# Layer tail of a hybrid decoder trunk: separate products, norms and MLP against one program that goes chunk by chunk

## The reference, cut to what matters

```python
x = x + g1 * rms_norm(m, norm_g[l, 1])                 # m = mixer output @ w_out
h = rms_norm(x, norm_g[l, 2]) * (1 + sc2) + sh2
x = x + g2 * rms_norm(jnp.square(relu(h @ w1)) @ w2, norm_g[l, 3])
# the next layer begins: h = rms_norm(x, norm_g[l+1, 0]) * (1 + sc1) + sh1;  h @ w_in
```

## Time and profile before

| What | us |
|---|---|
| Median of three runs | 3804.24 |
| The profiled execution, its own time | 3808.08 |
| Span of its trace, first to last instruction | 3806.4 |
| Product with `w_out`, layer 0 (1281.9 to 1380.0) | 98.1 |
| Norms behind it (1380.0 to 1473.1) | 93.1 |
| MLP of layer 0 (1473.1 to 2266.1) | 793.0 |
| Norms behind it (2266.1 to 2358.8) | 92.7 |
| Norms behind the `w_out` product of layer 1 | 93.4 |
| Final norm and output (3750.6 to 3806.4) | 55.8 |

### The profile page before, as it was taken

One profiled execution on the slowest core, in us unless ns is written; L12 is line 12 of the kernel. 1 busy time (PEld: TensorE's weight loads), 2 busy tenths in 40 slices (PEclk: granted clock), 3 DMA queues, 4 the chain that ended last, 5 costly groups with the idle time before them and its releaser, 6 DMA issues. The chain is left out here.

```text
span 3806.4 us, 43764 instructions
## 1 busy us (share of the span) xinstructions
PE 3190.1 (84%) x17509; PEld 2794.1 (73%) x17509; DVE 1407.3 (37%) x1513; ACT 880.2 (23%) x1083; POOL 761.3 (20%) x422
## 2 busy tenths in 40 slices
PE   4988888699587766999999984979693899999996
PEld 2973333299365666999999983958393899999996
DVE  4026641101693345322322335139316332232234
ACT  3016642100321213111111122013303111111112
POOL 1111111111000132211221223225023222122121
PEclk7999989899796777999999995989695999999997
DMA  5110025310432112111111111130312111111112
GB/s 198 56 51 8 1 72 178 116 50 28 132 95 75 50 53 86 41 42 44 44 39 44 44 64 71 43 108 0 100 33 94 56 44 39 44 44 39 44 44 94
DMA packets 216088, 238.36 MB, mean 63 GB/s; under 512 B 7779, under 2 KB 173079, under 8 KB 214837
## 3 DMA queue, kind: packets, MB, share of 16 engines
q1 hardware_dynamic: 210229, 219.14, 17.9%
q0 software_dynamic: 5120, 16.78, 1.4%
q10 hardware_dynamic: 656, 1.36, 0.1%
HBM read 207.74 MB, written 29.99 MB: 62 GB/s over the span
## 5 line engine op out<-in xcount | busy, mean ns | idle before, releaser
L771 POOL TENSOR_TENSOR mlp_w_lo<-mlp_w_raw,mlp_w_hi 128x1024 fp32r<-128x1024 f32 x128 | 316.1, 2470 | 1250.6 <-ACT mlp_w_hi L748 1250.6
L614 PE MATMUL PS<-mid_x_hi,mlp_w_hi 128*128 128x364 f32 x1536 | 509.8, 332 | 46.3 <-POOL mlp_w_lo L771 46.3
L614 PE MATMUL PS<-mlp_h_hi,mlp_w_hi 128*128 128x364 f32 x1536 | 507.3, 330 | 40.7 <-DVE mlp_h_lo L820 40.7
L615 PE MATMUL PS<-mid_x_lo,mlp_w_hi 128*128 128x364 f32 x1536 | 505.9, 329 | 0.0
L615 PE MATMUL PS<-mlp_h_lo,mlp_w_hi 128*128 128x364 f32 x1536 | 505.5, 329 | 0.0
L616 PE MATMUL PS<-mlp_h_hi,mlp_w_lo 128*128 128x364 f32 x1536 | 504.7, 329 | 0.0
L616 PE MATMUL PS<-mid_x_hi,mlp_w_lo 128*128 128x364 f32 x1536 | 504.4, 328 | 0.0
L823 DVE TENSOR_TENSOR M<-M,PS 128x1092 f32<-128x1092 f32 x128 | 165.4, 1292 | 558.2 <-PE PS L616 558.2
L614 PEld LDWEIGHTS PS<-mid_x_hi,mlp_w_hi 128*128 128x128 f32 x1536 | 289.7, 189 | 46.8 <-issue 46.8
L614 PEld LDWEIGHTS PS<-mlp_h_hi,mlp_w_hi 128*128 128x128 f32 x1536 | 289.9, 189 | 45.6 <-DVE mlp_h_lo L820 45.6
L748 ACT ACTIVATE mlp_w_hi<-mlp_w_raw 128x1024 fp32r<-128x1024 f32 x128 | 134.8, 1053 | 691.3 <-PE PS L616 668.5
(11 more groups left out here) (373 smaller groups left out, 5643.0 us busy)
## 6 DMA issues: line engine op xcount, KB each, us to landing
mlp_w_raw<-mlp_w SPq DMA_DIRECT2D x128, 512.0 KB
M<-cache_sb_k SPq DMA_DIRECT2D x64, 256.0 KB, 3.1
big<-cache_sb_v POOLq DMA_DIRECT2D x64, 256.0 KB, 3.5
hgrn_pairs_ada_w<-ada_w SPq DMA_DIRECT2D x24, 512.0 KB
x_scratch<-big SPq DMA_DIRECT2D x2, 4368.0 KB
x_mid<-x_scratch SPq DMA_DIRECT2D x2, 4368.0 KB
x_scratch<-x_mid SPq DMA_DIRECT2D x2, 4368.0 KB
setup_ada_w<-ada_w SPq DMA_DIRECT2D x16, 512.0 KB, 7.2
```

Source lines behind the costliest of these rows:

```text
L614: pe.matmul(out, hi, xh, start=first, stop=False)
L615: pe.matmul(out, hi, xl, start=False, stop=False)
L771: pool.tensor_tensor(wl[:, u % 2, :], raw[:, u % 2, :], wh[:, u % 2, :].bitcast(F32), ALU.subtract).then_inc(s_lo, 1)
```

## The change

`mlp_of_layer`, the `residual_norm` behind the MLP and the `dense` for `odd_w_in` are replaced by one program per layer, `trunk`, without a barrier inside. Its order of work on PE is: the `w_out` product in two halves of four slices, each half chunk by chunk; then eight groups of hidden and output slices, each chunk by chunk; then, in layer 0, the product with `odd_w_in` in three parts of four slices, each chunk by chunk. Four weight tiles are resident (`w_hi`, `w_lo` have four slots), so that four slices of one chunk are computed before the next chunk. A slice of one chunk (`tile8`) is 24 pairs into one bank, an output slice of a chunk 12 pairs; six banks go round, and banks 6 and 7 hold the sums and the spread factors of the norms. The two norms of a chunk are issued between the products of later chunks (`norm_step`), at written places. ACT and DVE have one written order in which the steps of the norms stand between the copies, the hidden slices and the weights. `x` and the hidden slices share one memory, and so the old `x` is loaded in three chunks at the start, and each chunk of the new `x` is stored on ACT's queue.

The core of the diff:

```diff
-def mlp(nc, core, tag, w1, w2, M):
+def trunk(nc, core, tag, l, w_out, w1, w2, w_next=None):
+        wh = sb("w_hi", [P, 4, 8 * P], F32R)
+        wl = sb("w_lo", [P, 4, 8 * P], F32R)
+        freed_g = [9, 10, 11, 12, 30, 32, 34, 36]
...
+            for u in range(2):
+                load_tile(u, w_out, u * P)
+            for c in range(NC3):
+                sp.dma_start(col(X, c), col(x_rows, c)).then_inc(s_x[0][c], 16)
+            for u in range(2, 8):
+                load_tile(u, w_out, u * P)
+            with sp.Fori(0, G) as g:
+                load_group(g)
...
+            def sums(j, n, c):
+                pe.wait_ge(s_tree[j][n], 2 * (c + 1))
...
+                for k in range(2):
+                    for b in range(4):
+                        q = pe.matmul(PS[0:TB, 6 + n, SUM_AT + 4 * c + b:SUM_AT + 4 * c + b + 1],
+                                      sq[:, k, b * TB:(b + 1) * TB], cols(core, "ones"), ...
+            def spread(j, n, c):
+                pe.wait_ge(s_rs[j][n], c + 1)
...
+                if phase == 3:
+                    if s == 4:
+                        sums(j, 1, 1)
+                    if s == 5:
+                        spread(j, 1, 1)
+                    if s == 6:
+                        sums(j, 0, 2)
+                    if s == 7:
+                        spread(j, 0, 2)
...
+            def tile8(bank, slot, c, after=None):
+                for k in range(KT):
+                    q = product(pe, PS[:, bank, 0:CW], wh[:, slot, k * P:(k + 1) * P], wl[:, slot, k * P:(k + 1) * P],
+                                XH[:, k, c * CW:(c + 1) * CW], XL[:, k, c * CW:(c + 1) * CW], k == 0, k == KT - 1)
+                    if k == 3 and after is not None:
+                        after(0)
+                q.then_inc(s_mm, 1)
...
+            def hidden_phase(g, c, first=False, step=None):
+                for i in range(4):
+                    if c == 0:
+                        pe.wait_ge(s_lo, g * 8 + (8 + i + 1))
+                    if first and i == 0:
+                        pe.wait_ge(s_xl[0], 2 * (c + 1))
...
+            def down_phase(g, c, step=None):
+                for f in range(8):
+                    if f == 0:
+                        pe.wait_ge(s_h, g * 12 + 4 * (c + 1))
...
+            for c in range(NC3):
+                out_phase(0, c)
+            for c in range(NC3):
+                out_phase(1, c, lambda s: norm_step(0, c, s))
+            for c in range(NC3):
+                hidden_phase(0, c, True, lambda s: norm_step(0, 3 + c, s))
+            for c in range(NC3):
+                down_phase(0, c)
+            with pe.Fori(1, G - 1) as g:
...
+                act.dma_start(col(x_rows, c), col(X, c)).then_inc(s_st[j][c], 16)
...
-        mlp_of_layer(nc, core, 0, core.even_w_out, M)
...
+            trunk(nc, core, "trunk0", 0, core.even_w_out, core.mlp_w1[0], core.mlp_w2[0], core.odd_w_in)
             odd_mixer(nc, core, "odd")
...
+            trunk(nc, core, "trunk1", 1, core.odd_w_out, core.mlp_w1[1], core.mlp_w2[1])
```

More of the change, by code:

```diff
@@ L742, in _ @@
         @block.scalar
         def _(act):
[L744 to L772, removed]
@@ new lines, in group @@
+            def group(g):
+                for c in range(NC3):
+                    for i in range(4):
+                        hidden(g, c, i)
+            for c in range(NC3):
+                dve.wait_ge(s_sh, c + 1)
+                dve.tensor_tensor(col(XL, c), col(M, c), col(XH, c).bitcast(F32), ALU.subtract).then_inc(s_sl, 1)
+            tree(0, 0, 0)
+            recip(0, 0, 0)
+            scaled(0, 0)
+            residual(0, 0)
+            tree(0, 1, 0)
+            tree(0, 0, 1)
@@ new lines, in _ @@
+            recip(0, 1, 0)
+            normed(0, 0)
+            recip(0, 0, 1)
+            low(0, 0, 0)
+            low(0, 0, 1)
+            scaled(0, 1)
+            residual(0, 1)
+            hidden(0, 0, 0)
+            tree(0, 1, 1)
+            hidden(0, 0, 1)
+            tree(0, 0, 2)
+            hidden(0, 0, 2)
+            recip(0, 1, 1)
+            normed(0, 1)
+            recip(0, 0, 2)
+            hidden(0, 0, 3)
+            low(0, 1, 0)
+            low(0, 1, 1)
+            scaled(0, 2)
@@ new lines, in _ @@
+            residual(0, 2)
+            hidden(0, 1, 0)
+            tree(0, 1, 2)
+            hidden(0, 1, 1)
+            hidden(0, 1, 2)
+            hidden(0, 1, 3)
+            recip(0, 1, 2)
+            normed(0, 2)
+            low(0, 2, 0)
+            low(0, 2, 1)
+            for i in range(4):
+                hidden(0, 2, i)
+            for c in range(NC3):
+                for f in range(8):
+                    down(0, c, f, True)
+            with dve.Fori(1, G - 1) as g:
+                group(g)
+                for c in range(NC3):
+                    for f in range(8):
+                        down(g, c, f)
@@ new lines, in _ @@
+            tree(1, 1, 0)
+            down(e, 2, 0)
+            tree(1, 0, 1)
+            down(e, 2, 1)
+            recip(1, 1, 0)
+            down(e, 2, 2)
+            down(e, 2, 3)
+            normed(1, 0)
+            recip(1, 0, 1)
+            down(e, 2, 4)
+            down(e, 2, 5)
+            low(1, 0, 0)
+            down(e, 2, 6)
+            low(1, 0, 1)
+            down(e, 2, 7)
+            scaled(1, 1)
+            residual(1, 1)
+            tree(1, 1, 1)
+            tree(1, 0, 2)
```

564 lines of the change are left out of this document (488 added, 76 removed).

## The result

The changed kernel takes 3593.73 us (median of four runs, 3588.66 to 3604.74), the kernel before 3805.89 us beside it: a ratio of 0.944, 95% interval 0.9418 to 0.9461. The forecast was 3603. The profiled run took 3591.43 us with a span of 3589.8.

A forecast was written before the change was run, and what follows sets the result against it. PE was taken to bound the products, and a chain of ACT, DVE, POOL and small PE steps the norms. 40.7 + 52.0 + 52.3 + 46.5 + 19.6 - 15.4 + 5.4 = 201 us off 3804.2 gave 3603, range 3560 to 3650.

The forecast's parts named there:

- Wait in each group: In each of the MLPs' 16 groups PE waited 2.54 us for DVE's `mlp_h_lo`; this goes, saving 40.7 us.
- restarts: After long waits PE starts at half clock: 13 pairs at 0.308 instead of 0.168 us, 1.8 us each.
- Norms behind `w_out`, layer 0: Norms after layer 0's `w_out` product: 14.8 us small matmuls, 22.7 waits, 3.6 clock; 41.1 left of 93.1, 52.0 saved.
- Norms and next product: Norms behind the first MLP, interleaved with the next input product: 46.2 us left of 92.7, 46.5 saved.
- The end: Last norms and output of the kernel: 36.2 us left of 55.8, 19.6 saved.
- Start: earlier by: At each tail's start the first weight tile waits for one chunk's input copies, not all eight: 4.6 us earlier.
- Start: wait for the third weight: At each tail's start three x loads precede the third `w_out` tile on SP: PE waits 10.5 us per layer.
- Sum of the tails: All savings in both layers, less 15.4 us lost at the starts: 201 us.
- the norms did not hide: Rival: norm chains hide wholly beside products and x loads share the queue; 111 us less, 3492 us; chance 0.08.
- A new wait in each group: Rival: MLP weight tiles come late, so 2.5 us per group stay; 41 us more, 3644 us; chance 0.13.
- The clock at half through the stretches: Rival: PE's clock stays half through the three norm stretches; 145 us more, 3748 us; chance 0.09.
- It did not fall between sets: Rival: waits at bank changes drop the clock, output slices run at half; 645 us more, 4248 us; chance 0.04.

The follow-up runs named there:

- chunk 1 early: The changed kernel with chunk 1's second-norm root, reciprocal, high and low parts moved ahead in ACT's and DVE's queues: 3575.6 us, 0.9382 of before.
- all moves: The changed kernel with x loaded behind the fourth `w_out` tile, chunk 1's and 2's norm steps earlier, POOL's subtractions behind DVE's remainder: 3556.1 us, 0.9336 of before.
- the run with the two apart: The changed kernel, but before the next input product POOL's third and fourth weight tiles wait for DVE's remainder of chunk 0: 3602.1 us, one run.
- the run on the end: The kernel with all moves, plus DVE's last-norm sum with x of chunk 1 split and put behind the last addition: 3549.1 us, 0.9327 of before.

## Why the prediction was right

Its steps against the profiled run; a pair is 672.33 / 4032 = 0.1667 us, so 864 pairs take 144.1 and 288 take 48.0:

| Step | predicted | measured |
|---|---|---|
| Wait in each group | 40.7 saved | 16 x (98.9 - 96.05) = 45.6, with two restarts |
| Norms behind `w_out`, layer 0 | 41.1 left | 197.17 - 144.1 - 8.9 = 44.2 |
| Norms and next product | 46.2 left | 59.33 - 48.0 + 180.87 - 144.1 = 48.1 |
| The end | 36.2 left | 55.58 - 48.0 + 32.34 = 39.9 |
| Start: earlier by | 4.6 each | 14.86 - 9.80 = 5.1, and 5.1 |
| Start: wait for the third weight | 10.5 each | 4.71, and 6.18 in layer 1 |
| Sum of the tails | 201 saved | 207.1 |

(8.9 are the wait of 4.71 and the two restarts at the tail's start, 2.6 and 1.6.)

The waits inside the norms came out as summed from the rows: 1.38 (1), 2.33 (2.4), 6.38 (6.3), 2.33, 10.62 (10.6); in the next product 5.42 (5), 5.84 (5.8) and 10.63. Their causes are shown in part: the order in ACT's and DVE's queues by the runs with chunk 1 early and with all moves, POOL beside DVE by the run with the two apart. What is left before chunks 1 and 2 (3.1 and 8.6 us) is argued to be the chain's own length; no run shortened it. The group wait is shown by putting it back. It gave 4.9 us more than foretold; 3.0 of them are the two restarts, the rest is open.

Three terms were mis-sized. *The start* took 270 GB/s for the loads of x, between 192 and 355. They ran at 367; the second row is two weight tiles behind them in the queue:

```profile
1271.00:1279.00 8.00, 8.00 (x34) 8.00 (x34) 7.72 (x2) 3.15 (x2) 4.43 (x1) 0.67 1.06 367
...
1279.50:1282.50 3.00, 2.00 (x12) 1.69 (x11) 0.00 (x0) 0.00 (x0) 0.00 (x0) 1.00 1.16 295
```

The first row is x alone: its 2.93 MB went in 2044 packets, all but 30 of 1456 bytes. 4.47 MB then take 12.2 us and not 16.6, which takes 4.4 of the 10.5 us away; the value next to the faster row was the right one. The step that failed is the reading of 192 GB/s as the rate of 512-byte pieces: it is the mean of a window of 2.6 us in whose first half little moved (at most 142 GB/s), and in whose last third the same pieces moved at over 300. *The end* left out that DVE does chunk 1's sum with x, 4.15 us, before the last addition; the run on the end moves it, and the stretch comes to the 29 us foretold. *The norms* were too cheap, by 3.1 us behind `w_out` and 1.9 behind the MLP, though their waits were right. A restart was counted for the long waits only; behind the short ones, of 1.38 and 2.33 us, the clock stood at half too:

```profile
1395.80:1399.20 3.40, 3.30 (x12) 2.82 (x10) 1.79 (x2) 0.06 (x1) 0.00 (x0) 0.50 0.00 0
1402.60:1406.00 3.40, 3.40 (x14) 3.36 (x13) 3.40 (x7) 0.00 (x0) 0.00 (x0) 0.51 0.00 0
```

At the 1.5 us of a restart in the run with the wait put back, an estimate, these two make up the 3.1 us. The start was some 11 us too dear, the norms and the end some 12 too cheap. That the sum came within 6 us is in part luck; that it is near 200 is not.

The rivals: the norms did not hide. By moving entries in the queues the start's wait, the two waits before a spread, half of chunk 1's and a fifth of chunk 2's could be hidden, 45 us of the 111 foretold for that case. A new wait in each group did not come, even with POOL's work doubled. The clock at half through the stretches shows as short dips; the mean is 0.91 to 0.93 there. It did not fall between sets: 672 us at 1.00 with 24 more sets in each group. The section of the Trainium skill that spoke for that rival (TensorE: Matmul & The Clock Gate, "A second HAM failure mode: psum-queue depth-cycling") tells of small idle times between sets. This trace has none in the MLP (PE busy for 672.33 of 672.33 us), so that cycling through banks alone did not bring them about here.

## What to carry to other kernels

Where every wait of a written order can be named with the queue entries ahead of the waiting step, the waits can be summed from durations in the old trace, here to 0.1 us for most and 0.4 for the others. What went wrong here is a transfer's rate read from a window that holds its start, work that stands in a queue ahead of the last step, and the clock behind short waits. When a stage is interleaved, ask of each remaining wait whether it is the chain's length or the order of two queues: moving a few entries gave 17.5 us in the tails without a new instruction. Cut runs into stages before comparing: the part that the change left alone moved by 23 us between runs.

## What the runs showed that was not expected

- In the run with the wait put back, PE stood 2.3 us in each of 16 groups of work at full rate. Behind six of these waits the clock stood at 0.5 for a stretch, at 1.5 us each (13 pairs in 3.60 us, mean clock 0.55); behind the others it stayed at 1.00. The sum of waits is then too low a price.
- Beside POOL, DVE can slow down over a whole stage and not only where two instructions collide: with POOL's work in the MLP doubled, DVE's 336 instructions there took 286.4 us and not 179.5, and the eight of a remainder before it 14.86 and not 4.3.
- x in pieces of 1456 bytes moved at 367 GB/s, no slower than whole rows (355); two queued weight tiles of 512-byte pieces moved at 295, where a window around a single one gave 192.
